# Two blocks of a network on one core: which inputs are multiplied unnormed, and where the norm's factor is applied

## What is computed

```python
def rmsnorm(x, w):                       # also rms_norm
    y = x * lax.rsqrt(jnp.mean(x * x, axis=-1, keepdims=True) + EPS)
    return y * w

# first block, after its mixers have given y
x = x + y @ w_out
h2 = rms_norm(x, norm2_w)
x = x + jnp.square(jax.nn.relu(h2 @ ffn_w1)) @ ffn_w2            # up1, down1

# second block
h = rmsnorm(x, norm_mix_pre)
rq, rk, rv, rg, gq, gk, gv, gg, ga, sq, sk, sv, gate_logits = split(h @ w_in)
o_ret = head_groupnorm(retention(rq, rk, rv)) * silu(rg)         # 4 heads
log_a = max(log_sigmoid(ga @ gla_w_alpha2 + b) / 16, -1)
o_gla = head_rmsnorm(gla(gq, gk, gv, log_a)) * silu(gg)          # 4 heads
o_swa = swa_sinks(sq, sk, sv, attn_sinks)                        # 16 heads
x = x + rmsnorm(sum_b(sigmoid(gate_b) * (o_b @ w_branch_b)) @ w_out, norm_mix_post)
h = rmsnorm(x, norm_ffn_pre)
f = (silu(h @ ffn_w_gate) * (h @ ffn_w_up)) @ ffn_w_down
x = x + rmsnorm(f, norm_ffn_post)
```

## Time and profile before

| what | value |
|---|---|
| median of 3 runs | 1927.37 us (1924.52 to 1928.87) |
| the profiled execution | 1925.15 us, its span 1923.4 us |
| mean granted PE clock | 0.979 |
| PE busy | 1844.2 us, 96% |
| PE weight load busy (beside PE) | 1444.6 us, 75% |
| DVE busy | 892.4 us, 46% |
| ACT busy | 497.4 us, 26% |
| GpSimd (POOL) busy | 932.7 us, 48% |

### The profile page before, as it was taken

The page is one execution under the profiler, slowest core; times in us unless marked ns, Lnnn a source line. Parts: engine busy times, 40 slices in busy tenths (PEclk is TensorE's granted clock), DMA queues, the critical chain, the costliest instruction groups (busy, mean ns, idle before and its releaser), DMA issues.

```text
span 1923.4 us, 22066 instructions
## 1 busy us (share of the span) xinstructions
PE 1844.2 (96%) x8468; PEld 1444.6 (75%) x8468; DVE 892.4 (46%) x1402; ACT 497.4 (26%) x982; POOL 932.7 (48%) x507
## 2 busy tenths in 40 slices
PE   7999989899999999999999999999999989999996
PEld 5785556788888877777887778677778768888885
DVE  6428753662046241444006274666654656305533
ACT  2125562120012001222013131455400232212221
POOL 5443123566666655455664452544466534444441
PEclk9999999999999999999999898999999999999998
DMA  5610101222222232122222112211122213222221
GB/s 180 212 57 26 46 23 66 74 102 99 99 99 93 94 110 88 66 78 88 95 99 71 61 66 73 92 67 66 62 92 90 85 55 110 95 94 97 99 99 55
DMA packets 47736, 164.51 MB, mean 86 GB/s; under 512 B 5504, under 2 KB 6720, under 8 KB 47249
## 3 DMA queue, kind: packets, MB, share of 16 engines
q1 hardware_dynamic: 44240, 156.62, 23.4%
q10 hardware_dynamic: 3393, 6.48, 1.2%
HBM read 160.10 MB, written 2.12 MB: 84 GB/s over the span
## 4 chain that ended last, share of the span: by engine, by line
PE 82%; DVE 10%; ACT 4%; issue 2%; POOL 1%; DMA 1%; SPq 0%; ACTq 0%; DVEq 0%; POOLq 0%
PE bank L691 81%; DVE tmp L1478 1%; DVE o_hi L1456 1%; PE bank L948 1%; DVE o_lo L1457 1%; POOL w_lo_t L2004 1%; DMA w_raw<-in_w 1%; DVE att_l_t L1782 1%; DVE att_l_t L1923 0%; DVE sq_sum L1473 0%; ACT sq L1141 0%; ACT L1105 0%; DVE tmp L1902 0%; DVE att_l_t L1921 0%; DVE x_sb L1969 0%
## 5 line engine op out<-in xcount | busy, mean ns | idle before, releaser
L2004 POOL TENSOR_TENSOR w_lo_t<-w_raw,w_hi_t 128x1024 fp32r<-128x1024 f32 x276 | 685.1, 2482 | 222.1 <-ACT w_hi_t L1174 204.2
L691 PE MATMUL bank<-h_hi,w_hi_t 128*128 128x512 f32 x1344 | 548.2, 408 | 32.0 <-POOL w_lo_t L2004 16.8
L2002 POOL TENSOR_SCALAR w_hi_t<-w_raw 128x1024 fp32r<-128x1024 f32 x213 | 229.7, 1078 | 700.7 <-PE bank L691 659.0
L691 PE MATMUL bank<-h_lo,w_hi_t 128*128 128x512 f32 x1344 | 530.8, 395 | 1.6 <-DVE h_lo L1539 0.9
L691 PE MATMUL bank<-h_hi,w_lo_t 128*128 128x512 f32 x1344 | 529.4, 394 | 0.0
L691 PEld LDWEIGHTS bank<-h_hi,w_hi_t 128*128 128x128 f32 x1344 | 256.2, 191 | 108.7 <-issue 44.0
L691 PEld LDWEIGHTS bank<-h_lo,w_hi_t 128*128 128x128 f32 x1344 | 256.4, 191 | 60.4 <-DVE h_lo L1506 4.0
L691 PEld LDWEIGHTS bank<-h_hi,w_lo_t 128*128 128x128 f32 x1344 | 255.8, 190 | 55.2 <-issue 0.5
L691 PE MATMUL bank<-hid_hi,w_lo_t 128*128 128x512 f32 x432 | 168.1, 389 | 0.0
L691 PE MATMUL bank<-hid_hi,w_hi_t 128*128 128x512 f32 x432 | 168.0, 389 | 0.0
L691 PE MATMUL bank<-hid_lo,w_hi_t 128*128 128x512 f32 x432 | 168.0, 389 | 0.0
(11 more groups left out here) (267 smaller groups left out, 2324.9 us busy)
## 6 DMA issues: line engine op xcount, KB each, us to landing
w_raw<-in_w SPq DMA_DIRECT2D x276, 512.0 KB, 3.2
y<-in_w SPq DMA_DIRECT2D x6, 512.0 KB, 6.3
x_sb<-in_x SPq DMA_DIRECT2D x4, 512.0 KB, 7.2
x_sb<-in_x ACTq DMA_DIRECT2D x2, 1024.0 KB, 5.6
alibi<-in_alibi SPq DMA_DIRECT2D x8, 256.0 KB, 5.3
out_y<-x_sb SPq DMA_DIRECT2D x8, 256.0 KB, 2.0
u_raw<-in_w SPq DMA_DIRECT2D x2, 512.0 KB, 6.2
toep<-table ACTq DMA_DIRECT2D x4, 256.0 KB
```

Source lines behind the costliest of these rows:

```text
L691: return pe.matmul(out, lhs, rhs, start=start, stop=stop, **kw)
L2002: pool.tensor_scalar(hi, raw, 1.0, 0.0, ALU.mult, ALU.add).then_inc(*did("w_hi", i))
L2004: pool.tensor_tensor(lo, raw, hi.bitcast(F32), ALU.subtract).then_inc(*did("w_lo", i))
```

## The change

- `n2` and `pre` join the unnormed keys. `u` stands inside `wout` and inside the second half of `down1`; `apply_h` goes. The chunks for `up1` get tiles of their own (`u2_hi`, and `u2_lo05` in the space of `att_l` and `att_pt`), those of `pre` use `h_hi`, `h_lo`.
- The norm of `n2` and of `pre` stands behind the matmuls of the first three blocks. `r_cols` for `pre` stands between the second and third slot of `rv`.
- Every output of these chunks gets the factor at evacuation. `up1`: DVE takes max(bank, 0) x factor, ACT squares and writes the high half, DVE subtracts (`hidden_low`). `rq`, `rk`, `gq`, `gk`, `wq`, `wk`, `ga`: evacuated by DVE with the factor, before by ACT. `rv`, `gv`, `wv`: ACT, scaled by the column. `rg`, `gg`: DVE writes bank x factor to `silu`, ACT takes the sigmoid of that, DVE multiplies in `ret_mean` and `gla_turn` (`silu_of`). `gate`: DVE writes bank x factor to `sig`, ACT takes the sigmoid in place.
- At the gated FFN, `residual` of chunk c + 1 stands before `u` of chunk c, and all squares stand before the first matmuls' step (and so before the weight casts on ACT).
- In a `together` step whose chunk is new, all names' products with the high half stand before the wait for the low half.

```diff
-                order.append(("sq", key, o))
+                run(([("u", key, o)] if key == "pre" else []) + [("sq", key, o)])
...
-        order.append(("sq", "n2", c))
-    order.append(("norm", "n2"))
-    order.append(("apply_h", "n2", "norm2"))
+        run([("u", "n2", c), ("sq", "n2", c)])
     part, ends = together([("up1", 0, c) for c in range(3)])
-    run([part(0, KD)] + ends)
+    run([("use_h", "n2"), part(0, KD), ("norm", "n2")] + ends)
...
-    order.append(("norm", "pre"))
-    order.append(("apply_h", "pre", "pre"))
     part, ends = together([("rq", 0), ("rk", 0), ("rq", 1)])
-    run([part(0, KD)] + ends + tm(("rv", 0), 4, 512))
+    rv = tm(("rv", 0), 4, 512)
+    run([("use_h", "pre"), part(0, KD), ("norm", "pre")] + ends + rv[:2] + [("r_cols", "pre")] + rv[2:])
...
     order.append(("norm", "post"))
+    order.append(("residual", "post", 0))
     for c in range(KD):
-        run([("residual", "post", c), ("u", "fpre", c)])
+        run([("residual", "post", c + 1)] * (c + 1 < KD) + [("u", "fpre", c)])
...
-    run([part(0, KD)] + sqs("fpre", KD) + [alone(0, KD), ("norm", "fpre")] + ends + end)
+    run(sqs("fpre", KD) + [("use_h", "fpre"), part(0, KD), alone(0, KD), ("norm", "fpre")] + ends + end)
...
-UNNORMED = ("n1", "fpre")
+UNNORMED = ("n1", "n2", "pre", "fpre")
...
                 elif key in ("rg", "gg"):
                     _, h, e = name
                     n = sig_at[name]
-                    act.wait_ge(*full(name))
+                    act.wait_ge(*evacuated(name))
                     if n >= 2:
-                        act.wait_ge(*evacuated(sig_user(n - 2)))
+                        act.wait_ge(*sig_free(n - 2))
                     functions("sigmoid")
-                    act.activation(sig[:, n % 2], ps(name)[:], ACT.Sigmoid).then_inc(*did("gate_s", name))
+                    act.activation(sig[:, n % 2], silu[:, e], ACT.Sigmoid).then_inc(*did("gate_s", name))
...
+        def silu_of(kind, h):
+
+            for e in range(2):
+                own("gate_s", (kind, h, e))
+                ins = dve.tensor_tensor(silu[:, e], silu[:, e], sig[:, sig_at[(kind, h, e)] % 2], ALU.mult)
+                ins.then_inc(*did("silu", (kind, h, e)))
+            own("silu", (kind, h, 1))
...
+                    if n == 0:
+                        own("rstd", "n2")
+                    dve.wait_ge(*full(name))
+                    dve.scalar_tensor_tensor(out=r1[:, n % 2], in0=ps(name)[:], scalar=0.0, in1=r_h[:], op0=ALU.max,
+                                             op1=ALU.mult).then_inc(*release(name))
+                    if c:
+                        hidden_low(half, c - 1)
+                elif key in ("rq", "gq", "rk", "gk"):
...
+                        ins = dve.tensor_tensor((kf if key[1] == "k" else qf)[:, h % 2], ps(name)[:], r_h[:], ALU.mult)
+                    ins.then_inc(*release(name))
+                    dve.wait_ge(*evacuated(name))
                 elif key in ("rg", "gg"):
-                    own("gate_s", name)
-                    dve.tensor_tensor(silu[:, e], ps(name)[:], sig[:, n % 2], ALU.mult).then_inc(*release(name))
+                    dve.wait_ge(*full(name))
+                    dve.tensor_tensor(silu[:, name[2]], ps(name)[:], r_h[:], ALU.mult).then_inc(*release(name))
                     dve.wait_ge(*evacuated(name))
+                elif key == "gate":
+                    dve.wait_ge(*full(name))
+                    dve.tensor_tensor(sig[:, sig_at[name] % 2], ps(name)[:], r_h[:], ALU.mult).then_inc(*release(name))
...
                 own("ret_d", h, 1)
+                silu_of("rg", h)
...
                                   gmask[:, None, :].to_broadcast([P, NT, P]), ALU.mult).then_inc(*release(("ga_s", h)))
+                silu_of("gg", h)
```

More of the change, by code:

```diff
@@ L457, in _program @@
     r1 = sa("r1", [P, 2, T])
+    u2_hi, u2_lo67 = sa("u2_hi", [P, KD, T], F32R), sa("u2_lo67", [P, 2, T], F32R)
+    u2_lo = [u2_lo05[:, c] for c in range(6)] + [u2_lo67[:, c] for c in range(2)]
     area.close()
@@ L650, in _program, with sig_free @@
     sig_at = {name: i for i, name in enumerate(sig_names)}
-    def sig_user(n):
+    def sig_free(n):
         name = sig_names[n]
-        return ("br",) + name[1:] if name[0] == "gate" else name
+        return evacuated(("br",) + name[1:]) if name[0] == "gate" else after("silu", name)
     TAB = ((0, 512), (512, 128), (640, 512), (1152, 512))
@@ new lines, in _ @@
+                xh, xl = u_of.get(seen_h, lin_src[src]) if src == "h" else lin_src[src]
+                blocks = [(k, names) for k in range(k0, min(k1, KD - 2))]
+                blocks += [(k, (name,)) for name in names for k in range(max(k0, KD - 2), k1)]
+                for k, some in blocks:
+                    fresh = src == "h" and ("h_ready", seen_h, k) not in chunks_seen
+                    if fresh:
+                        pe.wait_ge(*after("u_hi" if seen_h in UNNORMED else "h_hi", seen_h, k))
+                    else:
+                        x_chunk_ready(src, some[0], k)
+                    wsl = slice(k * P, (k + 1) * P)
+                    for name in some:
+                        i = SLOTS[name][0]
+                        mm(ps(name)[:], w_hi[:, RING[i], wsl], xh[k], k == 0, False)
+                        last = mm(ps(name)[:], w_lo[:, RING[i], wsl], xh[k], False, False)
+                        if not fresh:
+                            last = mm(ps(name)[:], w_hi[:, RING[i], wsl], xl[k], False, k == KD - 1)
+                            if k == KD - 1:
+                                fill(name, last)
+                                slot_free(i, name=name)
+                    if fresh:
+                        x_chunk_ready(src, some[0], k)
+                        for name in some:
+                            i = SLOTS[name][0]
+                            last = mm(ps(name)[:], w_hi[:, RING[i], wsl], xl[k], False, k == KD - 1)
+                            if k == KD - 1:
+                                fill(name, last)
+                                slot_free(i, name=name)
@@ L797, in _ @@
                     wsl = slice(k * P, (k + 1) * P)
[L798 removed]
+                    last = mm3(out[:], w_hi[:, RING[i], wsl], w_lo[:, RING[i], wsl], xh[k], xl[k],
                                k == 0, k == KD - 1)
@@ L1478, in scaled, with hidden_low @@
             return dve.scalar_tensor_tensor(out=dst, in0=src, scalar=w, in1=rstd(key), op0=ALU.mult, op1=ALU.mult)
+        def silu_of(kind, h):
[4 more added lines that the diff above has]
+            own("silu", (kind, h, 1))
+        def hidden_low(half, c):
+            own("hid_s", ("up1", half, c))
+            dve.tensor_tensor(hid1[1][:, c], r1[:, (half * HALF1 + c) % 2], hid1[0][:, c].bitcast(F32), ALU.subtract)\
+               .then_inc(*did("hid", "down1", half, c))
+            own("hid", "down1", half, c)
         for i, v in enumerate(EPS_VAL):
@@ L1600, in _ @@
                     _, half, c = name
-                    own("hid_s", name)
-                    if half == 1 and c == 0:
-                        dve.wait_ge(*full(("down1", 0, KD - 1)))
-                    if half == 0 and c == 0:
-                        dve.wait_ge(*full(("wout", KD - 1)))
-                    split(r1[:, (half * HALF1 + c) % 2], hid1[0][:, c], hid1[1][:, c], "hid", "down1", half, c)
+                    n = half * HALF1 + c
+                    if n == 0:
+                        own("rstd", "n2")
@@ L1617, in _ @@
                     dve.wait_ge(*full(name))
-                    dve.wait_ge(*evacuated(("gate", b, m)))
+                    own("gate_s", ("gate", b, m))
                     t = merged[:, m] if b == 0 else tmp[:, n % 2]
```

117 lines of the change are left out of this document (53 added, 64 removed).

## The result

The changed kernel takes 1931.7 us in the median against 1927.2: ratio 1.0024, 95% interval 1.0015 to 1.0033. It is 4.5 us slower; 9.3 were forecast (1936.5 - 1927.2). The profiled execution of the changed kernel (`after`) took 1937.0 us, the longest of its twenty, so its profile is no fair picture of the median. I profiled the same kernel once more (`after_again`, 1930.1 us), and read both. Their spans are 1935.1 and 1928.2 us at a mean granted clock of 0.973 and 0.976, that of the kernel before is 1923.4 at 0.979.

What follows compares the result with a forecast made beforehand. TensorE, busy 96%, bounds the kernel: 1925.2 - 1.9 - 1.5 - 4.7 + 0.5 + 0.7 + 9.6 + 6.7 = 1934.6, so a median of 1936.5 us was forecast; own range 1931.5 to 1942, 8 in 10 1925 to 1947.

Steps and rivals of the forecast that it cites:

- the gated linear attention: Heads 0 to 3: loss 9.6 us (2 to 19), from 6.7 of waits, 0.6 gained, 3.5 for the clock.
- the gated border: Gated FFN's input: chunks come faster and squares stand before weight casts; gain 4.7 us (3.0 to 6.4).
- the split: Attention output, third branch: VectorE splits only after gate 1, so TensorE leaves later; loss 6.7 us (2.8 to 10).
- the attention: Attention part: 13 evacuations enter VectorE's queue, results still early enough; loss 0.5 us (0 to 9).
- the pace of up1: First FFN's up-projection: evacuations moved to VectorE lie beside 5.44 us of TensorE work; cost nothing.
- the two early borders: Inputs of first FFN and second block: matmuls start before the norm, after a 3.86 us wait; gains 1.9 and 1.5 us.
- retention: Retention: two silu x sigmoid products before the sum of squares delay a mean matmul; loss 0.7 us.
- (a): Rival, chance 0.13: the clock stays up at heads 1 to 3 of gated linear attention; total 1922.3 us.
- (b): Rival, chance 0.20: VectorE no earlier, all heads fall, split and borders at half clock too; about 1948 us.
- (c): Rival, chance 0.16: new waits are short, 0.8 us a head, split 2.8, no further fall; 1925 us or little more.
- (d): Rival, no chance of its own: TensorE waits for the borders' third slot longer than 3.86 us, each us costing one.

Runs made afterwards that it cites:

- one_tile_borders: Changed kernel with the three side-by-side tiles at the first FFN's and second block's borders put back to one after another: 1918.1 us, ratio 0.9955.
- alone -6.3: Kernel before with only the gated FFN border's order changed (residual one chunk ahead, squares ahead of the first three tiles' products): 1920.1 us, ratio 0.9967.
- split_first: Changed kernel with the split of the sliding-window output put ahead of branch 2's two first gates: 1925.8 us, ratio 1.0001.
- gla_order: Changed kernel, gated linear attention: sigmoids behind the turned keys' copy, their products behind the state updates (heads 0 to 2): 1920.9 us, ratio 0.9976.
- three moves of a few lines: Changed kernel with the split ahead of the gates, gated linear attention reordered and border tiles one after another, together: 1903.1 us, ratio 0.9889.

## Why the prediction went wrong, point by point

The direction was right: slower, and each new wait came where it had been put. The size was forecast at twice what came. Against `after_again`, the execution nearer to the median, the gated linear attention was set 5.9 us too high, the gated border 1.6, the split 1.5 and the attention 0.7; the pace of up1, put at nothing, was 3.4 too low and the two early borders 1.6. Errors of both signs cancel here: without those that were too low the total would have come out at about nothing, so that the direction came right is partly luck.

**The gated linear attention (forecast 9.6, measured 6.3 and 3.7) is the step that failed: it added waits and falls of the clock as if all could come at once.** It put in 2.2 us at each of three heads, kept today's two falls of the clock whole, and added 3.5 us for a third one at head 2. The table above shows that they trade against each other: where the clock is down at head 2, head 3 waits 0.23 us instead of 2.90. Forecast were 6.7 us of waiting and 3.5 of clock. In `after` PE's idle time over the three heads has grown by 3.0 us and its busy time by 3.7; in `after_again` idle time by 5.2, busy time by -1.1; in the mean over all profiles 4.4 and 1.1. The order before makes the same trade, and one trace of it (0.89, 1.00, 0.76) looked like two sure falls and one sure escape. Why the clock falls at head 2 in some executions and not in others stays open.

The chain within a head was partly wrong as well. To PE's first kv product it was too long: VectorE's evacuation was placed well (7.5 us behind the turn, 8.9 before, 1.4 earlier where 1.2 was forecast), then came a table load that is not in that chain. Without it PE's idle time there should be 4.7 - 1.28 = 3.4 us; it is 3.15. But the forecast took its 2.2 us a head from the state updates, and these start 12.7 us behind the turn against 10.9 before: 1.8 later where 2.15 was forecast, since the two products in front of them took 2.40 us together. So the misplaced load explains little of the term. The Trainium skill's page "ScalarE: Activation LUTs", section "What ACT_TABLE_LOAD costs", would have added its drain of 1380 ns on top; the rows of `after` show neither load nor drain there.

**Both early borders (forecast -3.4, measured with the up1 tiles +1.1 and +1.6).** The wait of 3.86 us was right (4.00). Its half-clock stretch was a little short: eight to twelve matmuls at 0.43 us, where 1.6 us stood for eight. What was put at nothing without a reason is the place of the new tiles: it was taken as a matter of space, and it costs 3.1 of the 3.4 us in the pace of 29 tiles. And one question was not asked at all, whether the side-by-side block still earns its wait; no term of the sum depends on it, but `one_tile_borders` puts 14.3 us on it.

**The gated border (forecast -4.7, measured -6.4 and -6.3, alone -6.3).** The mechanism was right and the size low: the chunks came every 2.05 us (2.15 forecast), and PE's four blocks and the mean were done at 1579.5 in `after`, which is 1561.3 on the clock of the kernel before (18.2 us of delay so far), against 1563.0 forecast. PE idled 5.34 us ahead of the fourth block, where 6.3 were forecast.

**The split (forecast +6.7, measured 5.2 and 5.2 in the profiles).** Right in place and waiter (4.38 us of idling, 4.7 forecast), 1.5 us high in size. That the medians of `split_first` give the same 6.7 is chance.

**Evacuations in the attention (0.5) and in retention (0.7).** Small as forecast.

**The rivals.** (a), that the clock would stay up at all three heads, did not come in any profile. Nearest to it is `gla_order`, at heads 1 and 2 alone and by no idling rather than by longer idling: from the turn of head 0's keys to the last head's mean 154.8 us against 160.8 before, where (a) had 4.9 less. (b), (c) and (d) did not come: waits, split and third slot were near the forecast's lengths. The median lies in the range, and at the low edge of the forecast's own (1931.5 to 1942). The sum has a slip of 0.3 (1934.6 + 2.2 is 1936.8, not 1936.5). It also compared one execution with another and added 2.2 us, while a single execution of the changed kernel lies anywhere in 12 us.

## What to carry to other kernels

When a change makes inputs come earlier, look again at every arrangement that was made for late inputs: here it was a block of three tiles side by side, and leaving it in cost 14 us. When an evacuation moves to another engine, list what stands behind its consumer in both queues; three moves of a few lines took back more than the change had cost. Where the clock falls in one stage of a trace and not in its neighbour, take more than one profile before either is put into a sum, and add up the neighbouring stages: here 7 us at one head were 3 over three heads.

## What the runs showed of the hardware

- Two executions of one kernel differ by what the granted clock does in single stages: 44.75 and 37.89 us for the same 171 matmul rows of head 2 at 0.77 and 0.95, with head 3 at 26.02 and 30.12 us the other way round. With the order before it is 36.12 and 41.59 us at head 2, 28.36 and 19.87 at head 3. The Trainium skill, page "TensorE: Matmul & The Clock Gate", section "Part 1: The HAM clock gate", says that the monitor runs on its own time and so the same kernel meets it differently from run to run. It tells this of a kernel's start; these profiles agree, in the middle of the kernel too.
- Matmuls of one shape do not all run at one pace at full clock: 226.7 ns on the old chunks and on the hidden layer, 231.1 on the new chunks, 228.3 when their place was shifted by 32 bytes.
- In these kernels the load of a function table runs ahead of the wait for the sigmoid's input: 1117.92 against 1129.71 in `after`, 755.41 against 762.43 before.
